# Chunk 0 of a streaming encoder kernel: instruction order on five queues

## The reference

```
h = rmsnorm(x) * g;  u = h @ w_in          # 1024 -> 11 groups of 256 columns
a: y = a_b * conv3(a_c * a_x) * silu(a_g)
b: y = silu(layernorm(conv31(b_v * sigmoid(b_a)) + bias)) * silu(b_g)
c: y = (trailing means of c_u over 2, 4, 8, 16 rows - c_u) @ pool_w ... * silu(c_g)
x: y = softmax(x_q . mem_k) @ mem_v * silu(x_g)     # 4 heads, 256 memory rows
out = rmsnorm(x + concat(ya, yb, yc, yx) @ w_out)
```

## Time and profile before

| | us |
|---|---|
| median of three runs | 1472.85 |
| the profiled execution, its own time | 1474.04 |
| its span, first to last instruction | 1472.2 |
| PE busy in the span | 1430.6 |
| DVE busy | 1180.9 |
| ACT busy | 561.3 |
| POOL busy | 216.5 |
| mean granted TensorE clock | 0.996 of full speed |

### The profile page before, as it was taken

How to read it: one execution, slowest core, us unless ns; L and a number is a source line. 1 busy time by engine, 2 the same in 40 slices (tenths; PEclk the granted TensorE clock), 3 DMA queues, 4 the chain that set the end, 5 groups by cost and what they waited for, 6 DMA issues and landing times.

```text
span 1472.2 us, 32643 instructions
## 1 busy us (share of the span) xinstructions
PE 1430.6 (97%) x11766; PEld 1224.2 (83%) x11766; DVE 1180.9 (80%) x3087; ACT 561.3 (38%) x1237; POOL 216.5 (15%) x180
## 2 busy tenths in 40 slices
PE   5898999999999999999999999999999999999997
PEld 4687888888888888888888888888888888888875
DVE  6896696987959697895959789695968869596897
ACT  7775243333324333332434233243423423242342
POOL 0062011111101111110111111011111111111111
PEclk9999999999999999999999999999999999999999
DMA  9976455555364556446355654635565463545663
GB/s 265 259 268 211 170 174 188 200 199 199 114 239 146 185 199 227 172 128 252 118 197 188 228 185 139 251 107 203 182 215 187 160 247 91 216 168 199 231 206 118
DMA packets 127522, 280.88 MB, mean 191 GB/s; under 512 B 12297, under 2 KB 69309, under 8 KB 127485
## 3 DMA queue, kind: packets, MB, share of 16 engines
q1 hardware_dynamic: 127485, 280.40, 55.3%
HBM read 221.86 MB, written 58.49 MB: 190 GB/s over the span
## 4 chain that ended last, share of the span: by engine, by line
PE 87%; DVE 6%; DMA 2%; issue 2%; ACT 2%; SPq 2%; POOL 0%; ACTq 0%; DVEq 0%
PE u L621 20%; PE u L622 19%; PE u L623 19%; PE sps L621 5%; PE sps L623 4%; PE sps L622 4%; PE qps L621 4%; PE qps L623 4%; PE qps L622 4%; PE ops L730 2%; DVE z L1603 1%; DMA ring<-wo_split 1%; DMA w_hl<-in_w_in 1%; DVE w_hl L1584 1%; SPq L397 1%
## 5 line engine op out<-in xcount | busy, mean ns | idle before, releaser
L621 PE MATMUL u<-h_hi,w_hl 128*128 128x256 f16 x2816 | 770.1, 273 | 2.8 <-DVE w_hl L1584 2.7
L622 PE MATMUL u<-h_lo,w_hl 128*128 128x256 f16 x2816 | 769.1, 273 | 0.0
L623 PE MATMUL u<-h_hi,w_hl 128*128 128x256 f16 x2816 | 769.0, 273 | 0.0
L1603 DVE SCALAR_TENSOR_TENSOR z<-glu,cst,z 128x256 f32<-128x256 f32 x960 | 412.3, 499 | 0.5
L621 PEld LDWEIGHTS u<-h_hi,w_hl 128*128 128x128 f16 x2816 | 276.4, 98 | 47.4 <-issue 7.9
L623 PEld LDWEIGHTS u<-h_hi,w_hl 128*128 128x128 f16 x2816 | 276.1, 98 | 32.5
L622 PEld LDWEIGHTS u<-h_lo,w_hl 128*128 128x128 f16 x2816 | 276.2, 98 | 32.2 <-issue 0.7
L1050 ACT ACTIVATE gate<-u,inv 128x256 f32<-128x256 f32 x192 | 79.5, 466 | 113.8 <-PE u L623 113.5
L2107 POOL TENSOR_TENSOR sa<-cu 128x540 f32<-128x540 f32 x16 | 30.0, 1877 | 548.6 <-ACT cu L1050 477.9
L621 PE MATMUL sps<-ring,y_hi 128*128 128x512 f32 x256 | 101.8, 398 | 2.3 <-POOL y_lo L2092 2.1
L621 PE MATMUL qps<-ring,y_hi 128*128 128x512 f32 x256 | 101.8, 398 | 0.5 <-DMA ring<-wo_split 0.5
(11 more groups left out here) (317 smaller groups left out, 1978.5 us busy)
## 6 DMA issues: line engine op xcount, KB each, us to landing
ring<-wo_split SPq DMA_DIRECT2D x248, 512.0 KB, 7.8
ob<-in_x_prompt SPq DMA_DIRECT2D x34, 512.0 KB, 4.2
probs_turned<-probs SPq DMA_DIRECT2D x128, 128.0 KB, 2.4
pt<-probs_turned SPq DMA_DIRECT2D x32, 512.0 KB, 3.6
out<-ob SPq DMA_DIRECT2D x32, 512.0 KB, 3.1
rows_turned<-rows SPq DMA_DIRECT2D x112, 128.0 KB, 2.4
w_hl<-in_w_in SPq DMA_DIRECT2D x20, 512.0 KB, 7.3
wo_split<-ring SPq DMA_DIRECT2D x16, 512.0 KB, 5.0
```

What stands on the lines that cost most here:

```text
L621: nc.tensor.matmul(out, a_hi, b_hi, start=first, stop=False)
L622: nc.tensor.matmul(out, a_hi, b_lo, start=False, stop=False)
L623: return nc.tensor.matmul(out, a_lo, b_hi, start=False, stop=last)
L1603: ins = nc.vector.scalar_tensor_tensor(z[:, c, 0:n], glu[:, c, k:k + n], w, z[:, c, 0:n], ALU.mult, ALU.add)
```

## The change

Only the order inside chunk 0 changes; no instruction is added or taken away.

- PE: `sample_transposes` goes behind `project(0, N, "c_u")`.
- ACT: `cu_out` goes ahead of `sample_hi`; the pieces of W_out, `w_square(20)`, `w_square(21)`, the `w_high` from 17 on, `exps` and `probs_hi` are put in another order.
- DVE: the lower weight halves and scales stand ahead of taps; 11 taps instead of 6 stand behind `probs_lo(0, N, 1)`; `w_scale(10)` stands ahead of `probs_lo(0, N, 0)`; `both_rms` stands ahead of `z_stats` and `z_norm`.
- SP: `probs_leave(0, 0, N)` goes between the loads of pieces 11 and 12.

```diff
 (first_sync, SP: this loop stood in one piece, 4 to 15, ahead of first_sync)
+                for p in range(RAW, PIECES - RAW):
+                    keep(p - RAW)
+                    load_piece(p)
                 probs_leave(0, 0, N)
+                for p in range(PIECES - RAW, PIECES):
+                    keep(p - RAW)
+                    load_piece(p)
                 for p in range(PIECES - RAW, PIECES):
                     keep(p)
                 probs_arrive(0, 0, N)
 (first_chunk, PE)
-                sample_transposes()
                 memory_product(5)
                 project(0, N, "c_u")
+                sample_transposes()
                 memory_product(6)
 (first_chunk, ACT)
                 w_high(11)
+                cu_out(0, N)
                 sample_hi()
                 w_square(18)
-                cu_out(0, N)
                 w_high(12)
...
                 w_high(15)
-                for k in range(2, 5):
-                    piece_hi(k)
                 w_high(16)
+                piece_hi(2)
+                piece_hi(3)
+                w_high(17)
+                w_square(20)
+                exps(0, N, 0)
+                piece_hi(4)
+                w_square(21)
                 piece_hi(5)
-                exps(0, N, 0)
-                for k in range(6, 8):
-                    piece_hi(k)
-                w_high(17)
+                w_high(18)
+                piece_hi(6)
+                w_high(19)
+                d_high(0, N)
+                piece_hi(7)
+                probs_hi(0, N, 0)
                 piece_hi(8)
...
                 act.wait_ge(wsq_ok.sem, FT)
                 scaled_out(0, N, "a_g", gate[:, 2, :, 0:N], ACT.Silu, ag_ok)
+                piece_hi(9)
+                exps(0, N, 1)
+                piece_hi(10)
+                raw_keep(0)
+                w_high(20)
+                piece_hi(11)
+                w_high(21)
+                piece_hi(12)
+                piece_hi(13)
+                probs_hi(0, N, 1)
+                piece_hi(14)
                 piece_hi(15)
-                raw_keep(0)
-                exps(0, N, 1)
-                for k in range(20, 22):
-                    w_high(k)
-                probs_hi(0, N, 1)
                 b_gate(0, N)
 (first_chunk, DVE; the list after the change, from tap 16 on)
                 taps(0, N, 16, 17)
                 keys_lo(0)
                 value_scale(0)
                 w_low(14)
                 values_lo(0)
                 w_low(15)
                 taps(0, N, 17, 18)
                 w_scale(9)
                 va_out(0, N)
                 softmax_max(0, N, 0)
                 w_low(16)
                 conv_a_taps(0, N)
                 w_low(17)
                 softmax_rcp(0, N, 0)
                 pool_diff(0, N)
                 ab_out(0, N)
                 w_low(18)
                 w_scale(10)
                 probs_lo(0, N, 0)
                 softmax_max(0, N, 1)
                 w_low(19)
                 d_low(0, N)
                 ya_out(0, N)
                 w_low(20)
                 taps(0, N, 18, 19)
                 softmax_rcp(0, N, 1)
                 w_low(21)
                 taps(0, N, 19, 20)
                 probs_lo(0, N, 1)
-                taps(0, N, 25, 31)
+                taps(0, N, 20, 31)
                 yx_out(0, N)
+                both_rms(nxt[0][0])
                 z_stats(0, N)
                 z_norm(0, N)
-                both_rms(nxt[0][0])
                 rows_scale(*nxt[0], after=2)
```

More of the change, by code:

```diff
@@ L447, in _ @@
                 sp.dma_start(dst[0, 0].rearrange("(t p) h d -> p t (h d)", p=P), kv[:, :, off:off + GW]).then_inc(kv_in.sem, 16)
-            for p in range(RAW, PIECES):
-                keep(p - RAW)
-                load_piece(p)
             def store_states(k, outs):
@@ L1325, in first_chunk @@
                 w_high(15)
-                for k in range(2, 5):
-                    piece_hi(k)
                 w_high(16)
-                piece_hi(5)
-                exps(0, N, 0)
-                for k in range(6, 8):
-                    piece_hi(k)
-                w_high(17)
-                piece_hi(8)
[L1335 to L1346, removed]
+                piece_hi(2)
[5 more added lines that the diff above has]
+                w_square(21)
+                piece_hi(5)
+                w_high(18)
[4 more added lines that the diff above has]
+                probs_hi(0, N, 0)
+                piece_hi(8)
                 act.wait_ge(wsq_ok.sem, FT)
                 scaled_out(0, N, "a_g", gate[:, 2, :, 0:N], ACT.Silu, ag_ok)
-                piece_hi(15)
-                raw_keep(0)
-                exps(0, N, 1)
-                for k in range(20, 22):
-                    w_high(k)
-                probs_hi(0, N, 1)
+                piece_hi(9)
[9 more added lines that the diff above has]
+                piece_hi(14)
+                piece_hi(15)
                 b_gate(0, N)
@@ L1819, in first_chunk @@
                 taps(0, N, 10, 11)
+                for k in range(9, 11):
+                    w_low(k)
+                w_scale(6)
                 pool_weights_lo()
                 taps(0, N, 11, 13)
-                for k in range(9, 11):
-                    w_low(k)
+                w_low(11)
                 taps(0, N, 13, 14)
-                w_scale(6)
+                sample_lo()
                 taps(0, N, 14, 15)
-                w_low(11)
-                sample_lo()
-                taps(0, N, 15, 16)
@@ L1830, in first_chunk @@
                 w_scale(7)
                 w_low(12)
[L1832 to L1836, removed]
+                taps(0, N, 15, 16)
+                w_scale(8)
+                w_low(13)
+                taps(0, N, 16, 17)
                 keys_lo(0)
-                w_scale(8)
                 value_scale(0)
-                taps(0, N, 20, 21)
+                w_low(14)
@@ L1841, in first_chunk @@
                 values_lo(0)
+                w_low(15)
+                taps(0, N, 17, 18)
+                w_scale(9)
                 va_out(0, N)
                 softmax_max(0, N, 0)
-                w_low(15)
-                taps(0, N, 21, 22)
+                w_low(16)
+                conv_a_taps(0, N)
+                w_low(17)
+                softmax_rcp(0, N, 0)
                 pool_diff(0, N)
-                w_low(16)
-                w_scale(9)
-                softmax_rcp(0, N, 0)
@@ L1850, in first_chunk @@
-                conv_a_taps(0, N)
-                taps(0, N, 22, 23)
-                w_low(17)
                 ab_out(0, N)
+                w_low(18)
+                w_scale(10)
                 probs_lo(0, N, 0)
                 softmax_max(0, N, 1)
-                w_low(18)
-                taps(0, N, 23, 24)
                 w_low(19)
-                taps(0, N, 24, 25)
+                d_low(0, N)
                 ya_out(0, N)
-                d_low(0, N)
-                w_scale(10)
+                w_low(20)
@@ L1863, in first_chunk @@
+                taps(0, N, 18, 19)
                 softmax_rcp(0, N, 1)
-                for k in range(20, 22):
-                    w_low(k)
+                w_low(21)
+                taps(0, N, 19, 20)
                 probs_lo(0, N, 1)
-                taps(0, N, 25, 31)
+                taps(0, N, 20, 31)
                 yx_out(0, N)
+                both_rms(nxt[0][0])
                 z_stats(0, N)
                 z_norm(0, N)
-                both_rms(nxt[0][0])
                 rows_scale(*nxt[0], after=2)
```

## The result

The changed kernel takes 1482.72 us (median of 4 runs, 1480.3 to 1483.3), the kernel before 1472.66 (4 runs on the same chip, 1472.01 to 1474.01). The ratio is 1.0064, 95% interval [1.0047, 1.0081]: slower, as forecast, but by about 10 us in the medians and 8.2 us between the two profiled executions (1482.22 against 1474.04), where 4.4 were forecast. 1482.72 lies above the range of 1471.5 to 1481.

A forecast was written before the change was run, and what follows sets the result against it. Chunks 1 to 14 are PE-bound, so chunk 0's delay reaches the end: 3.5 (late `mix`) + 0.1 (clock) + 0.8 (zt) = 4.4 us slower, 1478.4 from 1474.04, less 1.2 for the median: 1477.2 us, range 1471.5 to 1481.

The forecast's parts named there:

- Part 1: c_u projection ahead of the transposes on PE: 4.35 us wait and 1.46 us slow clock go, sums 7.8 us earlier.
- Part 2: Chain to the probabilities' return that `attend(0,0)` waits for: PE stands some 15 us, `mix` starts 3.5 us late.
- sums and turn: Head of the chain: PE's sums at 102.5, then `w_scale(10)`, `probs_lo` and block transpose on DVE, done at 105.95.
- out-DMA: SP's four DMAs of the first pair's probabilities, ahead of the second exponentials: 3.7 us, landed at 109.65.
- ACT's halves: ACT behind the second exponentials: `piece_hi(10)` and `raw_keep(0)` at 0.53 us each, `w_high(20)` 1.13, done at 115.1.
- DVE's link to the reciprocals: `w_low(20)`, one tap and `softmax_rcp(0,N,1)` on DVE beside POOL's pieces: 2.3 to 4.2 us, taken as 3.5.
- The clock: PE's low clock behind its wait at `attend(0,0)`: even with before except for `attend` itself, 0.1 us slower.
- Part 3: Lower weight halves ahead of taps on DVE, and the rest of the reordering: costs nothing.
- Part 4: `both_rms` ahead of `z_stats` on DVE: zt ready 3.2 us later, PE stands 0.8 us, from 0 to 1.5.
- A: Rival: the c_u move's gain stays, return leaves before PE needs it, kernel faster at 1468.2 us; chance 0.11.
- B: Rival: the chain is shorter and all comes out even, 1470 to 1475.7 us, middle 1474; chance 0.21.
- C: Rival: the last pieces' loads land late, `piece_hi(15)` waits 2 to 4 us more, 1480 to 1482 us; chance 0.13.

The follow-up runs named there:

- e5_part1: Kernel before with only the c_u projection put ahead of the sample's transposes on PE and `cu_out` ahead of `sample_hi` on ACT: 1471.76 us, ratio 0.9973 to before.
- e1: Changed kernel with the return of the first pair's probabilities issued on SP behind `keep(13)` instead of `keep(15)`: 1481.10 us, ratio 1.0047 to before.
- e2: Changed kernel with `w_scale(10)` on DVE behind `probs_lo(0, N, 0)` and `softmax_max(0, N, 1)` instead of ahead: 1479.56 us, ratio 1.0040 to before.
- e9_small: Changed kernel with POOL's share of W_out's pieces 11 to 13 cut to 16 of 512 columns: 1480.84 us, ratio 1.0049 to before.
- e4_fill: Changed kernel with 160 extra matmuls of unused result on PE ahead of `attend(0, N, 0)`: 1479.61 us, ratio 1.0038 to before.
- e10_rms: Changed kernel with `both_rms` put back behind `z_stats` and `z_norm` on DVE: 1481.11 us, ratio 1.0051 to before.
- e3: Changed kernel with tap 18 on DVE behind `softmax_rcp(0,N,1)` and `w_low(21)` instead of ahead: 1480.94 us, ratio 1.0045 to before.
- e7: Changed kernel with the edits of e1 and e2, plus further reordering on SP, DVE and ACT and `both_rms` back behind `z_norm`: 1471.36 us, ratio 0.9980 to before.
- e6: Kernel of e1 with a DVE wait behind tap 23 until POOL's first `y_low` is done: 1480.03 us, ratio 1.0032 to before.
- e8: Kernel of e7 with a DVE wait behind tap 22 for POOL's first `y_low`: 1469.73 us, ratio 0.9970 to before.

## Why the prediction was wrong

- **Part 1** held: the 4.35 us and the slow product are gone, and the sums came 0.9 us later than forecast, 6.9 us ahead of before instead of 7.8. Of this, PE's wait for `va_out` was 0.92 us where 0.5 were taken for two places, the fourth memory product started 0.2 us later, and the transposes took 0.64 us where 0.45 were taken. PE reached `attend(0,0)` at 114.2, forecast 113.5 (the forecast's own terms add up to 113.7). e5_part1 shows that alone it is a gain.
- **Part 2, the mechanism**, held: `attend(0,0)` is set by the return, that by the stored pieces, those by the second softmax, that by the first pair's DMA, and that by `w_scale(10)`. e1 and e2 each took one link out and moved the return by 4.5 and 2.6 us.
- **Part 2, the sum** is what failed. The forecast had `attend` at 129.1, it started at 132.07. Link by link, measured less forecast: sums and turn +0.9, out-DMA +0.2, exponentials 0, ACT's halves -0.1, **DVE's link to the reciprocals +2.0** (5.5 us where 3.5 were taken between bounds of 2.3 and 4.2), `probs_hi` and pieces 0, POOL and SP +0.3, return -0.3: together 3.0. The failed step is the one that reads "the first is 1.2 us alone and 2.0 beside POOL's pieces, the tap 0.8 alone and 1.9 beside them". It took the contended rows as the upper end, and gave `softmax_rcp`, whose operations are tiny, no contended price at all. One tap (two instructions) took 2.91 us beside three pieces of POOL in a row, and the 128x4 operation waited about 1.07 us of its 1.22. e9_small takes POOL's work away and the link falls to 2.4 us. Both prices stood in the trace of before, in rows that the forecast did not use, on DVE and on POOL:

```profile
89.25 2.94 DVE L1603 SCALAR_TENSOR_TENSOR z<-glu,cst,z 128x256 f32<-128x256 f32 x2
...
97.40 1.09 DVE L1573 TENSOR_SCALAR w_scl<-w_exp 128x2 int32<-128x2 int32 x1
...
98.53 0.16 DVE L1619 TENSOR_SCALAR st<-st 128x4 f32<-128x4 f32 x1
...
86.96 6.38 POOL L2097 TENSOR_TENSOR ring<-rows,ring 128x512 fp32r<-128x512 f32 x4 [0.99 <-ACT ring L1116]
...
96.95 1.51 POOL L2097 TENSOR_TENSOR ring<-rows,ring 128x512 fp32r<-128x512 f32 x1 [0.73 <-ACT ring L1116]
```

A tap beside several pieces in a row took 2.94 us, and a 128x2 operation beside one piece 1.09 us, where the same one takes 0.17 to 0.22 alone. `softmax_rcp` itself was short there (0.16 us) because it fell behind the end of a piece (98.46), not because it is safe beside one. With these rows the link would have been 5.4 to 6.2 us (an estimate: low half 1.3 to 2.0, tap 2.9, the 128x4 operation 1.1, reciprocal 0.1 to 0.2).
- **The clock** was the second mis-sized term: 0.1 us was taken, on the ground that it was low before as well. From `attend`'s start to `mix` it took 1.43 us where 0.9 were taken, and the stretch from `mix` to W_out's pieces took 0.5 us more than before (8.18 us against 7.65), since 6 us were worked at the 1.2 GHz level instead of 3.4. That is 1.06 us in all. With the 1.7 us that before had already lost it makes 2.8, and e4_fill gives back 2.35 us with an `attend` that starts 0.43 us later, 2.8 as well. The low level did not last equally long behind each wait, as the 0.1 us took for granted.
- **Part 3** held: PE waits for no tap and no weight half.
- **Part 4** held: 0.8 forecast, 0.68 waited, 0.63 given back by e10_rms.

The sum then closes, for the profiled executions: 4.4 forecast, 3.0 more from the chain, 1.0 more from the clock and 0.1 less for zt give 8.3, against the 8.43 us by which chunk 1 starts later.

Of the 5.5 us by which the median of 1482.72 missed 1477.2, 3.8 are in this sum. The other 1.7 are in the step from an execution to the median: the forecast took 1.2 us off 1474.04, and the changed kernel's execution (1482.22) lies 0.5 us under its median. No run explains this difference.

Of the rivals, A and B did not come: a chain made shorter than forecast was needed for both. C came nearest in time (1480 to 1482), but for another reason: piece 15's load did not bind in the changed kernel (ACT ran pieces 14 and 15 without a gap at 123.36), it stood 1 to 2 us behind the link that did, and showed itself when that was shortened (e3, e9). The range was too narrow because its high end had DVE's link at 4.2 us, from rows with one piece of POOL beside an operation, and nothing for the clock. The high ends together did reach 8.3 us, but only with 1.5 us for piece 15's load, which did not come, and with 0.8 and 0.9 us for the two DMAs, which came within 0.3 us of the forecast: that this total equals the measured sum is chance.

The Trainium skill (SBUF — State Buffer, SBUF: two separate sides) says of the port pair that VectorE and GpSimd share that it is an exclusive lock and that the one that comes second waits for the whole instruction of the other. The 128x4 operation of 1.22 us beside POOL and of 0.15 to 0.17 us without agrees with it. The 6.58 us of one POOL operation, asked for in the middle of 22 tap instructions of 0.4 us each, go beyond one instruction's wait.

## What to carry to other kernels

When a wait of the busiest engine is removed, follow the next transfer it needs back through every queue, and price each small operation on that chain by what the sharing engine does at that moment, not by its own length: here the reorder put POOL's three subtractions beside DVE's reciprocals, and an operation of 0.15 us took 1.22. An instruction that waits, left ahead of that transfer in a queue (`w_scale(10)` ahead of `probs_lo`, `keep(15)` ahead of the return), gives an early engine's gain away; `w_scale(10)` moved behind was worth 2.6 us. And a wait that can't be removed costs the clock on top: matmuls of no use in it gave 2.4 and 2.6 us back.

## What was unexpected of the hardware

- A GpSimd subtraction of 128x512 that takes 1.27 us took 6.58 us (e1) and 5.73 us (e7) while VectorE ran 22 scalar_tensor_tensor instructions without a gap, and 1.27 us again when VectorE stood still (e6, e8). In before the same subtraction took 1.63 us inside a run of 12, and in after GpSimd's pieces go on at 1.57 us each with VectorE the one held off (two tap instructions 2.91 us instead of 0.87). Why one or the other is held is open.
- A 128x4 tensor_scalar on VectorE: 1.22 us beside GpSimd, 0.15 to 0.17 alone, the same in after, e1, e2 and e3 (1.22, 1.22, 1.22, 1.25).
- The same return DMA took 4.7 to 7.0 us from issue to PE's start (4.7 in after, 5.2 in e1, 5.9 in before, 6.2 in e9, 7.0 in e5).
- The granted clock came back after 6.0 us of work behind a wait of 17.8 us, and in before, behind waits of 1.3 and 2.0 us, after 3.4 us of work at the low level. The length of the wait does not order these: 4.7 us of work in e1 (wait 12.7), 4.9 in e7 (6.3), 3.9 in e8 (4.9) and 5.3 in e5 (4.0).
